# State-space mixer in an inference step: chunk rows sent before the norm, and results turned in TensorE instead of through DRAM

## The reference

```python
h = rmsnorm(x, mix_norm[layer])
ug = h.reshape(b, n, N_GROUPS, GROUP_CH)              # 64 groups of 16 channels
x_re = einsum('bngc,gpc->bngp', ug, bb_re)            # 64 complex states per group
x_im = einsum('bngc,gpc->bngp', ug, bb_im)
# s[n] = lam * s[n-1] + x[n], complex, over the 512 positions
y = einsum(s_re, c_re) - einsum(s_im, c_im)
y = gelu(y + d * h)
out = (y @ w_glu_v) * sigmoid(y @ w_glu_g)            # x = x + out
```

## Time and profile before

| | |
|---|---|
| median of three runs | 2057.05 us (2052.8 to 2058.31) |
| profiled execution | 2054.37 us, span 2052.7 us |
| TensorE busy | 1997.8 us, 97% |
| VectorE busy | 1284.7 us, 63% |
| ScalarE busy | 810.6 us, 39% |
| mean granted clock of TensorE | 0.974 |
| stage of the mixer, before the dense gate products | 417 to 534 us |

### The profile page before, as it was taken

The page is one execution under the profiler, slowest core; times in us unless marked ns, Lnnn a source line. Parts: engine busy times, 40 slices in busy tenths (PEclk is TensorE's granted clock), DMA queues, the critical chain, the costliest instruction groups (busy, mean ns, idle before and its releaser), DMA issues.

```text
span 2052.7 us, 41181 instructions
## 1 busy us (share of the span) xinstructions
PE 1997.8 (97%) x17318; PEld 1909.5 (93%) x17318; DVE 1284.7 (63%) x1797; ACT 810.6 (39%) x1255; POOL 153.3 (7%) x264
## 2 busy tenths in 40 slices
PE   8999999969999999999999999999999999999999
PEld 7999999958999999999999999998566799999998
DVE  5445476776348848566785775754774438657474
ACT  5222222221225525344452443544664335435252
POOL 3002002022100000000000000000036200000000
PEclk9999999975899999999999999999999999999999
DMA  6332234873342223331423232232146532322322
GB/s 148 88 97 85 81 92 117 241 155 89 109 154 83 83 83 124 99 97 53 134 95 121 86 111 77 82 105 57 42 130 169 172 103 83 124 83 91 116 73 73
DMA packets 266160, 215.75 MB, mean 105 GB/s; under 512 B 45572, under 2 KB 238626, under 8 KB 265986
## 3 DMA queue, kind: packets, MB, share of 16 engines
q1 hardware_dynamic: 253312, 190.15, 31.4%
q10 hardware_dynamic: 5970, 12.50, 1.9%
q0 software_dynamic: 6704, 10.63, 1.9%
HBM read 197.38 MB, written 12.43 MB: 102 GB/s over the span
## 4 chain that ended last, share of the span: by engine, by line
PE 90%; DVE 5%; ACT 3%; issue 2%; DMA 1%; SPq 0%; ACTq 0%; DVEq 0%; POOLq 0%
PE ps L2403 25%; PE ps L2332 25%; PE ps L2431 24%; PE ps L2345 3%; PE ps L2736 1%; PE ps L2742 1%; PE ps L2839 1%; PE ps L2945 1%; PE ps L2978 1%; PE ps L3101 1%; PE ps L3150 1%; PE ps L3115 1%; PE ps L2922 1%; DVE xl L1571 1%; DVE wl L1620 0%
## 5 line engine op out<-in xcount | busy, mean ns | idle before, releaser
L2332 PE MATMUL ps<-xh,wh 128*128 128x260 f32 x1120 | 296.2, 286 | 1.8 <-DVE xl L1571 1.4
L2332 PE MATMUL ps<-xl,wh 128*128 128x260 f32 x1120 | 292.2, 283 | 0.0
L2431 PE MATMUL ps<-xoh,wh 128*128 128x260 f32 x992 | 281.7, 284 | 1.3 <-DVE sq L1787 1.3
L2431 PE MATMUL ps<-xoh,wl 128*128 128x260 f32 x992 | 281.5, 284 | 0.0
L2431 PE MATMUL ps<-xol,wh 128*128 128x260 f32 x992 | 281.0, 283 | 0.0
L2403 PE MATMUL ps<-xh,wh 128*128 128x260 f32 x872 | 229.0, 284 | 0.7 <-DVE wl L1620 0.7
L2403 PE MATMUL ps<-xl,wh 128*128 128x260 f32 x872 | 227.1, 283 | 0.0
L2332 PE MATMUL ps<-xh,wl 128*128 128x260 f32 x1120 | 226.1, 284 | 0.0
L1041 ACT ACTIVATE wh<-rw 128x1024 fp32r<-128x1024 f32 (+1 forms) x135 | 138.8, 1029 | 218.6 <-PE ps L2403 151.7
L2332 PEld LDWEIGHTS ps<-xh,wh 128*128 128x128 f32 x1120 | 212.2, 189 | 6.7 <-issue 4.0
L964 ACT ACTIVATE wh<-raw 128x1024 fp32r<-128x1024 f32 (+1 forms) x90 | 100.5, 1116 | 285.3 <-PE ps L2332 267.8
(11 more groups left out here) (534 smaller groups left out, 4258.3 us busy)
## 6 DMA issues: line engine op xcount, KB each, us to landing
rw<-ffn_w_gate SPq DMA_DIRECT2D x33, 1024.0 KB, 5.4
rw<-ffn_w_up SPq DMA_DIRECT2D x33, 1024.0 KB, 8.3
rw<-ffn_w_down SPq DMA_DIRECT2D x12, 2048.0 KB, 8.1
raw<-ffn_w_gate SPq DMA_DIRECT2D x22, 512.0 KB, 3.8
raw<-ffn_w_up SPq DMA_DIRECT2D x22, 512.0 KB, 3.8
raw<-ffn_w_down SPq DMA_DIRECT2D x16, 704.0 KB, 4.9
rw<-ffn_w_down SPq DMA_DIRECT2D x6, 1536.0 KB, 6.7
cb<-cache_ckv SPq DMA_DIRECT2D x72, 128.0 KB, 3.9
```

The costliest lines, as they stand in the source:

```text
L2332: got = mm(ps[0:width, bank + half, 0:HALF], w[par_][:, k * width:k * width + width], src[:, k0 + k, half * HALF:half * HALF + HALF], star ...
L2431: got = mm(ps[:, bank + mat, T0], w[:, cols], src[:, j, k, :], start=first and k == 0 and m == 0 and s == 0, stop=k == 3 and m == 1, skip_ ...
```

## The change

- The prompt rows go out before the norm: in the last feed-forward products ScalarE scales tile `d` by its gain into `ta` and stores it; VectorE makes the eighth tile. `rows_in` loads come when the feed-forward products are done, and VectorE multiplies the loaded rows by the reciprocal deviation (`row_rstd`, 64 values a partition, picked out of PSUM).
- The new tokens' input products become a pass of their own (`sample_inputs`), with the last prompt chunk as a ninth column, behind the eight tiles; so the scan leaves out the last state, and GpSimd computes it (`fin`).
- The tap loads wait for the first half of that pass. The chunks are kept in another order, and the state in one tile `xsr`.
- `outputs(s)` takes two tiles of channels at once, with operands swapped. The result has chunks on the partitions.
- gelu writes to memory, TensorE turns it with eight transposes (`turned_rows`) into PSUM, and ScalarE and VectorE split it from there. Loads and stores through DRAM are gone.
- The first gate product is done in three parts between the outputs (`gate_values`); the two `keep_busy` before it are gone.

```diff
+            def rows_out(d):
+                if d >= 2:
+                    act.wait_ge(r_out[d % 2], R_0[d % 2] + 16 * (d // 2))
+                own(run(ta[:, d % 2, 0:SEQ].rearrange("p (i m b) -> p i m b", i=L, m=NBK),
+                        x[:, d, 0:SEQ].rearrange("p (b m i) -> p i m b", m=NBK, i=L), ACT.Copy,
+                        scale=gain[:, GAIN["s5"] + d:GAIN["s5"] + d + 1]))
+                act.dma_start(dr_u[d].rearrange("g c i n -> (g c) (i n)"), ta[:, d % 2, 0:SEQ]).then_inc(r_out[d % 2], 16)
...
             sp.wait_ge(w_used, at["glu"])
+            for t in range(3):
+                rows_in(t)
+            sp.wait_ge(s_us, US_0 + 1)
+            sp.dma_start(dr_u[KD - 1].rearrange("g c i n -> (g c) (i n)"), ta[:, 1, 0:SEQ]).then_inc(r_out[1], 16)
+            for t in range(3, KD - 1):
+                rows_in(t)
...
             def tap_rows(half):
-                sp.wait_ge(s_x, KD // 2 * (half + 1))
+                sp.wait_ge(s_x, KD + KD // 2 * (half + 1))
...
-            def gate_rows(t):
...
+            own(tt(by_own, ps[:, 6, :].rearrange("p (n i) -> p n i", i=L), own_step.unsqueeze(1).to_broadcast([P, NCH, L]), ALU.mult))
+            own(V.tensor_reduce(row_rstd.rearrange("p (m b) -> p b m", m=NBK), by_own.rearrange("p (b m) i -> p b m i", m=NBK), AX.X, ALU.add))
+            tt(us[:, :, :], us[:, :, :], ps[:, 7, 0:NB].unsqueeze(1).to_broadcast([P, KD, NB]), ALU.mult).then_inc(s_us, 1)
+            for t in range(KD):
+                dve.wait_ge(r_in[t % 4], RI_0[t % 4] + 16 * (t // 4 + 1))
+                tt(ush[:, place(t), :], ush[:, place(t), :], row_rstd.unsqueeze(1).to_broadcast([P, 8, NCH]), ALU.mult).then_inc(s_u, 1)
...
+            def carried_turns():
+                pe.wait_ge(s_s0, 64)
+                pe.wait_ge(s_xe, KD - 1)
...
+            def sample_inputs(t):
+                if t == 0:
+                    pe.wait_ge(s_ct, 2)
+                    pe.wait_ge(r_w, RW_0 + 48)
+                for q in range(QP):
+                    for r in range(2):
+                        for h in range(2):
+                            c = (QP * t + q) * (NB + 1)
+                            got = mm(ps[NS * h:NS * h + NS, r, c:c + NB + 1], wsh[:, 8 * t + 2 * q + h, r * NS:r * NS + NS],
+                                     usm[:, 8 * t + 2 * q + h, :], start=True, stop=True, skip_group_check=True)
+                got.then_inc(s_x, 1)
+            def outputs(s):
+                pe.wait_ge(s_sc, 2 * s + 2)
+                if s % 2 == 0:
+                    pe.wait_ge(r_tsh[s // 2], RTSH_0[s // 2] + 16 * L)
...
+                for q in range(QP):
+                    for h in range(2):
+                        for e in range(2):
+                            t, n = 2 * s + e, 2 * q + h
+                            mm(ps[NCH * e:NCH * e + NCH, bank + h, q * P:q * P + P], ush[:, place(t).start + n, :],
+                               tsh[:, 8 * t + n, :, :].rearrange("p j c -> p (j c)"), start=q == 0, stop=False, skip_group_check=True)
+                for r in range(2):
+                    for q in range(QP):
+                        for h, e in ((0, 0), (1, 1), (0, 1), (1, 0)):
+                            rows, n = slice(NS * h, NS * h + NS), QP * (2 * s + e) + q
+                            got = mm(ps[NCH * e:NCH * e + NCH, bank + h, q * P:q * P + P], xsr[rows, n, r, :, :].rearrange("p m b -> p (m b)"),
+                                     ctc[rows, r, n, :, :].rearrange("p j c -> p (j c)"), start=False, stop=r == 1, skip_group_check=True)
                 got.then_inc(s_yp, 1)
+            def turned_rows(s):
+                pe.wait_ge(xn_rdy, XN["glu"] + 2 * s + 2)
+                if s >= 1:
+                    pe.wait_ge(xl_rdy, GEN["glu"] + 2 * s)
+                for j in range(L):
+                    got = turn(ps[:, TURNED_BANK + j // 4, j % 4 * P:j % 4 * P + P], turned_y[s % 2][:, j * P:j * P + P])
+                got.then_inc(s_tp, 1)
...
             for t in range(KD):
                 chunk_inputs(t)
+            carried_turns()
+            for t in range(KD):
+                sample_inputs(t)
+            pe.wait_ge(s_xe, KD)
             sample()
+            for s in range(2):
+                outputs(s)
+                turned_rows(s)
+            pe.wait_ge(w_lo, g0 + 1)
+            pe.wait_ge(s_q7, 1)
+            gate_values(0, KD // 2)
+            outputs(2)
+            turned_rows(2)
+            outputs(3)
+            pe.wait_ge(s_q7, 2)
+            gate_values(KD // 2, KD - 2)
+            turned_rows(3)
+            gate_values(KD - 2, KD).then_inc(w_used, 1)
...
             def first_tiles(step):
-                if step in (6, 9):
-                    lo_out((6, 9).index(step))
+                if step == 3:
+                    lo_out(0)
+                elif step == 7:
+                    lo_out(1)
+                elif step == 8:
+                    new_low(0)
+                    los(g0)
...
-                by_step = x[:, d, 0:SEQ].rearrange("p (c i) -> p i c", i=L)
+                by_step = x[:, d, 0:SEQ].rearrange("p (b m i) -> p i m b", m=NBK, i=L)
```

More of the change, by code:

```diff
@@ L666, in block @@
             def block(m, b0, b1):
-                return xs[:, :, lo:hi, 0, b0 + 1:b1 + 1] if m == NBK - 1 else xs[:, :, lo:hi, m + 1, b0:b1]
+                return xs[:, :, lo:hi, 0, b0 + 1:min(b1 + 1, NB8)] if m == NBK - 1 else xs[:, :, lo:hi, m + 1, b0:b1]
             def advance(dst, src, coef, w):
@@ L1281, in _ @@
             half = KD // 2
[L1282 to L1285, removed]
+            act.wait_ge(r_out[0], R_0[0] + 16 * half)
+            act.wait_ge(r_out[1], R_0[1] + 16 * half)
+            gelu(0)
+            hi_out(0)
+            gelu(1)
+            act.wait_ge(s_q5, 1)
+            run(xh[:, 0:half, SEQ:TOK], ysb[:, 0:half, :], ACT.Copy).then_inc(s_q6, 1)
+            hi_out(1)
+            his(g0)
+            gelu(2)
             hi_out(2)
+            gelu(3)
+            run(xh[:, half:KD, SEQ:TOK], ysb[:, half:KD, :], ACT.Copy).then_inc(s_q6, 1)
             hi_out(3)
-            for t in range(half, KD):
-                gelu(t)
-                if t == half:
-                    his(g0)
-                elif t >= half + 2:
-                    hi_out(t - 2)
-            act.wait_ge(s_q5, 1)
-            act.wait_ge(s_yp, KD)
-            run(xh[:, :, SEQ:TOK], ysb, ACT.Copy).then_inc(s_q6, 1)
             his(g0 + 1)
-            hi_out(KD - 2)
-            hi_out(KD - 1)
             act.wait_ge(s_fp, 2)
@@ L2719, in chunk_inputs @@
                 got.then_inc(s_x, 1)
-            def outputs(t):
-                pe.wait_ge(s_sc, t + 1)
-                if t % 4 == 0:
-                    pe.wait_ge(r_tsh[t // 4], RTSH_0[t // 4] + 16 * L)
-                if t == 0:
-                    pe.wait_ge(s_xe, KD)
-                elif t == 3:
+            def carried_turns():
+                pe.wait_ge(s_s0, 64)
+                pe.wait_ge(s_xe, KD - 1)
+                for j in range(4):
+                    got = turn(ps[:, STATE_BANK, j * P:j * P + P], s0r[:, j, :])
+                got.then_inc(s_tr, 1)
@@ new lines, in turned_rows, with gate_values @@
+            def turned_rows(s):
[5 more added lines that the diff above has]
+                got.then_inc(s_tp, 1)
+            def gate_values(k0, k1):
+                for k in range(k0, k1):
+                    pe.wait_ge(xl_rdy, GEN["glu"] + k + 1)
+                    for m, (w, srcs_) in enumerate(((wh, (xh, xl)), (wl, (xh,)))):
+                        for half in range(2):
+                            for src in srcs_:
+                                got = mm(ps[:, half, 0:HALF], w[g0 % 2][:, k * P:k * P + P], src[:, k, half * HALF:half * HALF + HALF],
+                                         start=k == 0 and m == 0 and src is xh, stop=k == KD - 1 and m == 1)
+                return got
```

275 lines of the change are left out of this document (125 added, 150 removed).

## The result

The changed kernel takes 2032.94 us (median of four, 2031.29 to 2034.15), the kernel before 2055.6 us beside it: ratio 0.9889, interval 0.9872 to 0.9906, 22.7 us less. The forecast was 2030 us with a range of 2019 to 2048. Another set of four of the same kernel (label e5_again) gave 0.9899 (0.9878 to 0.9921).

What follows compares the result with a forecast made beforehand. Bound: TensorE in the state-space mixer, slow-clocked or waiting, until the first gate product ends. That end moves from 533.8 to 506.8, 27.0 us less: 2054.4 - 27.0 = 2027.4, plus 2.7 for the runs' median, so 2030; range 2019 to 2048.

Steps and rivals of the forecast that it cites:

- input side wins nothing for the outputs: Rival, chance 0.10: row loads, new tokens' scatter or tap loads later, outputs 0 start at 461 as before; 22 less, 2035.
- Row stores by ScalarE "hidden": Last feed-forward products: seven unnormalised tiles go out by ScalarE at about 1.09 us each, hidden; uncovered they cost 7 x 1.1.
- First rows ready at 425.5, input products with them: Input side: first normalised row tile at 425.5 us, input products starting then instead of at 433.3.
- Scan at 431.4: After ScalarE's fourth copy at 431.3, VectorE's scan starts at 431.4 us rather than 441.0.
- Scan priced equal, bounds 0 to +1 us per half: VectorE's scan: same operations, slightly fewer elements, new memory order of the state; equal price, 0 to +1 us per half.
- Outputs 0 released by a tap load, not by VectorE: First output products wait for the eighth tap load, not the scan, and start at 456.0 us instead of 461.1.
- Prices of the output products: Two tiles together: tap part 3.7 us, state part 3.85 at 1.2 GHz; 7.6 instead of 14.4, and 3.8 at 2.4.
- The rival of quarters in pairs: Rival, chance 0.11: array quarters overlap only in pairs, state part of the outputs costs 7.4 us; 16.5 less, 2040.5.
- the other side, halves that do not overlap: Rival, chance 0.06: array halves do not overlap in output products, a pair costs 14.4 us; 12.2 slower, 2069.
- Clock low until the middle of the first gate half: TensorE at 1.2 GHz from outputs 0 to half the first gate half (5.2 us, ending 488.1), then 2.4 GHz.
- the rival with 0.06: Rival, chance 0.06: clock rises already inside outputs 0, 5 us after its start; VectorE's scan binds at 483; 33 less, 2024.
- From outputs 2 to the second gate product 17.7: Outputs 2 and 3, gelu, transposes and remaining gate parts at 2.4 GHz, from 489.1 to 506.8 us.

Runs made afterwards that it cites:

- ordered-parts kernel: Changed kernel with output products of one part of the array all before the next, instead of alternating by record; one run, 2054.62 us.
- fifteen fillers: Changed kernel plus fifteen `keep_busy` products: four before outputs 0, nine before the first gate half, two before the last quarter; 2035.09 us, 0.9905.

## Why the prediction was right, step by step

Direction and range held, and so did the prices of the output products, which carry the gain, but the number is partly luck. Outputs 0 came 5.3 us later than forecast (461.28, not 456.0), and from there to the second gate product it took 49.0 us, not 50.8. The gain of 22.7 us is close to that of the rival with 0.10, "input side wins nothing for the outputs" (outputs 0 at 461, 22 less), and 4.3 short of the sum's 27.0; the time lies only 2.9 us above 2030 because the median of before was 1.4 lower this time (2055.6, not 2057.05). One reading of the rows was off without effect: the clock falls in three of the forty slices of the earlier trace rows, the ninth to the eleventh, not in two.

- **Row stores by ScalarE "hidden": failed.** The cover named, ScalarE's idle time, was there; the strided copies took 1.25 us each, not 1.1, and cost nothing. What was missed is their DMA issue: the first two took 0.38 us, the third stands behind a 4 MB load on the same queue and holds ScalarE for 12.65 us, so its next high part of the weights and its next square come late and TensorE stands 2.7 us between 390 and 410 (1.9 for the square, 0.8 for the low part that VectorE makes from the high one). Eight profiles with this order end feed-forward between 422.4 and 426.6 us, the four with the load moved between 419.4 and 420.4 (before: 420.75). Taking the load away gives 4.6 us in the median.
- **First rows ready at 425.5, input products with them: failed, 432.36.** 1.7 of it is the later feed-forward end. GpSimd's clears and copies stood at this place before too (2.37 us for the copies, 3.37 now); after the change the eighth tile and what follows it lie beside them, and they slow three VectorE operations from 0.71, 0.69 and 0.69 us to 2.08, 1.10 and 1.09, and delay the reciprocal by 2.2 of the 3.8 us that it is late (425.01, said 421.2). TensorE, which had stood since 423.6, was granted 0.50 from 426 to 432: the spread took 2.32 us where 1.0 was said, and the last products of the taps and the second pair of fillers also ran at that level before the input products. With the clears on ScalarE the way from feed-forward end to input products was 5.4 us, against 9.9 and 8.5.
- **Scan at 431.4: failed by 6, 437.35,** all of it inherited: from the first input product to the scan 5.0 us, said 5.9.
- **Scan priced equal, bounds 0 to +1 us per half: failed.** VectorE's steps lose 2.3 us between 442 and 446.5 and 0.9 at 451.5, both beside GpSimd's sum for the new tokens. Before, five of its six operations lay between 429.4 and 435.5 us, ahead of the scan, and only the last beside it (one pair of steps took 1.63 us there, so the 0.9 was in the price already). Now they wait for the transposed carried states and start at 441.87; the forecast moved them past the scan's start without pricing what they lie beside. The Trainium skill, "SBUF — State Buffer", Who interferes with whom, says that a VectorE instruction with two inputs in SBUF contends with a GpSimd instruction that reads SBUF, through a shared read interface. The rows agree: 0.42 us becomes 0.73 beside `TENSOR_TENSOR`, and stays 0.42 where these products are left out.
- **Outputs 0 released by a tap load, not by VectorE: failed**, by little. The new tokens' pass started at 441.01, where 436.1 was said; its first half ran at 2.4 GHz in 4.0 us (the clock fell at 446), and the tap loads left at 445.05, not 440.6. (The prediction's own prices, four tiles of 0.93 us from 436.1, give 439.8.) Adding the forecast's own 15.7 us gives 460.7, the issue of the eighth load (451.73) and 8.2 us to landing 459.9; VectorE's second group ended at 461.23. The rival "input side wins nothing for the outputs" had this place right (461), and a late tap load was among its reasons, but VectorE released it.
- **Prices of the output products: right.** The tap part took 3.68 us at 1.2 GHz, said 3.7; a pair at 2.4 GHz 3.9 us (470.05 to 473.93), said 3.8. No run shows the whole state part at 1.2 GHz. gelu 1.09 (said 1.3), transposes 1.09 (1.1), high 1.02, low 1.23. The rival of quarters in pairs and the other side, halves that do not overlap, are refuted by these rows and by the ordered-parts kernel. The rule of the Trainium skill that had been weighed, "TensorE: Matmul & The Clock Gate", Part 3, would make the tap part 5.1 us at 1.2 GHz; 3.68 was measured. What "TensorEngine Tiling (Array Packing)", Tiling Modes, says in the Trainium skill, that tiles load and multiply independently, agrees with the rows (62 ns a record alternating against 104 one after another, 31 against 95).
- **Clock low until the middle of the first gate half: failed**, in both directions. It rose inside outputs 0 (0.64 in 466 to 467, then 1.00), the rival with 0.06; but TensorE then stood from 476.2 to 485.03 and the gate half ran at 1.2 GHz (5.6 us, 5.2 said). The early rise gained little, because VectorE's second scan runs without a wait from 466.6 to 495.8 and holds the gate half and outputs 2 (the gate half, at 1.2 GHz, ended 0.3 us ahead of it): 29.7 us from outputs 0 to outputs 2, forecast 33.1. The path is VectorE from 437 to 490.9 us.
- **From outputs 2 to the second gate product 17.7: 19.4.** All steps came as said up to 507.5; the last quarter then ran at 1.2 GHz, 2.8 us instead of 1.3, after 2.5 us of standing. In the second trace of the same kernel it ran at 2.4 GHz, 1.5 us, after the same 2.5 us, and outputs 2 to the second gate product took 18.2: this step was right in one execution and 1.3 off in the other.
- **Behind it, nothing: right** (+0.4, less than executions of one kernel differ there).

Balance: 5.3 late, 3.5 won to outputs 2, 1.7 lost behind, 0.4 after: 3.9 of 27.0 missing, 23.1 left (from unrounded times).

The lost clock can't be won back in this kernel with the fifteen fillers (0.9889 without, 0.9905 with).

## What to carry to other kernels

A DMA issue belongs to the price of a moved step: look at what stands in front of it on the same issuing engine's queue; a busy share of that engine says nothing of it. When TensorE's products are halved, ask next which engine fed them: here VectorE's scan released the first output products already before the change, and what a faster TensorE gains ahead of the next result of the scan is given back there. And look at GpSimd work that a change shifts in time for the VectorE operations it now lies beside.

## What the runs showed of the hardware that was not expected

- Behind a load of 4 MB, issued in 0.81 us, the next DMA issue on that engine took 12.65 us (13.38 in another run); with the load issued by GpSimd, 0.37. GpSimd's own issue of it took 2.76 us. Stores on the queue ahead of the load took 0.38 us.
- VectorE beside GpSimd: a `TENSOR_SCALAR` of 512 elements 0.71 and 2.08 us, `TENSOR_TENSOR` of 512 elements 0.69 and 1.10, of 256 elements 0.42 and 0.73. The kind of operation matters: the 2.08 us stood beside a `MEMSET` of 1.81 us, and in the kernel before a `TENSOR_TENSOR` of 512 elements beside the same `MEMSET` (418.50, inside 418.01 to 419.82) took 0.69. Whether the loser waits or both are slowed no row decides.
- Output products in parts of the array, alternating against one after another: halves that share their rows are 1.7 times faster (62 and 104 ns a record at 2.4 GHz), quarters 3.1 times (31 and 95 ns), loads included.
- After the same 2.5 us of standing TensorE's clock fell within the next product in one execution of a kernel and stayed at 2.4 GHz in another.
